# A hybrid attention step in fp32: the second feed-forward network's last six output blocks, walked one token half at a time

## The reference, cut to what matters

```python
def rmsnorm(x, g):
    y = xf * lax.rsqrt(jnp.mean(xf * xf, axis=-1, keepdims=True) + RMS_EPS)
    return (y * g).astype(x.dtype)

h = x + 0.5 * swiglu(rmsnorm(x, g_ffn1), w1g, w1u, w1d)
h = h + mix                      # attention, not touched here
h = h + 0.5 * swiglu(rmsnorm(h, g_ffn2), w2g, w2u, w2d)
y = rmsnorm(h, final_norm)
```

## Time and profile before

| | |
|---|---|
| Median of 3 runs | 1061.3 us (1061.2, 1061.3, 1063.53) |
| Profiled execution, its own time | 1062.71 us |
| Its span in the trace | 1060.9 us |
| TensorE busy, share of the span | 98% |
| VectorE, ScalarE, GpSimd busy | 79%, 51%, 8% |
| Granted TensorE clock, mean | 0.994 of full |

### The profile page before, as it was taken

The page is one execution under the profiler, slowest core; times in us unless marked ns, Lnnn a source line. Parts: engine busy times, 40 slices in busy tenths (PEclk is TensorE's granted clock), DMA queues, the critical chain, the costliest instruction groups (busy, mean ns, idle before and its releaser), DMA issues. The chain is left out here.

```text
span 1060.9 us, 19168 instructions
## 1 busy us (share of the span) xinstructions
PE 1039.9 (98%) x7698; PEld 1008.7 (95%) x7698; DVE 835.1 (79%) x1257; ACT 539.8 (51%) x929; POOL 86.7 (8%) x84
## 2 busy tenths in 40 slices
PE   9999999999999999988999999999999999999996
PEld 9999999999999999977888889999999999999996
DVE  6999988999878463377777766699998899987744
ACT  7536645666455443344344444544664666645532
POOL 0000000000000034022322102200000000000022
PEclk9999999999999999999999999999999999999998
DMA  5222223223231335220112212213222322223122
GB/s 210 82 80 93 107 82 117 81 87 113 80 120 41 100 114 198 69 86 1 51 50 71 75 41 73 87 40 120 106 94 81 116 84 98 102 80 120 60 61 90
DMA packets 22663, 94.45 MB, mean 89 GB/s; under 512 B 2928, under 2 KB 6000, under 8 KB 16048
## 3 DMA queue, kind: packets, MB, share of 16 engines
q1 hardware_dynamic: 22576, 93.23, 25.4%
HBM read 88.24 MB, written 4.98 MB: 88 GB/s over the span
## 5 line engine op out<-in xcount | busy, mean ns | idle before, releaser
L808 PE MATMUL acc<-c_hi,w_lo 128*128 128x288 f32 x952 | 282.0, 296 | 0.0
L808 PE MATMUL acc<-c_hi,w_hi 128*128 128x288 f32 x952 | 281.1, 295 | 0.0
L808 PE MATMUL acc<-c_lo,w_hi 128*128 128x288 f32 x952 | 277.6, 292 | 0.0
L1564 DVE TENSOR_TENSOR w_lo<-raw,w_hi 128x1024 fp32r<-128x1024 f32 (+3 forms) x161 | 176.4, 1096 | 57.0 <-ACT w_hi L1149 54.3
L808 PEld LDWEIGHTS acc<-c_lo,w_hi 128*128 128x128 f32 x952 | 180.8, 190 | 0.0
L808 PEld LDWEIGHTS acc<-c_hi,w_hi 128*128 128x128 f32 x952 | 179.1, 188 | 0.2
L808 PEld LDWEIGHTS acc<-c_hi,w_lo 128*128 128x128 f32 x952 | 178.6, 188 | 0.0
L1149 ACT ACTIVATE w_hi<-raw 128x1024 fp32r<-128x1024 f32 (+3 forms) x161 | 145.5, 904 | 38.3 <-PE acc L943 17.2
L1297 ACT ACTIVATE comb<-acc 128x288 f32<-128x288 f32 x200 | 82.4, 412 | 151.4 <-PE acc L808 147.4
L1564 DVE TENSOR_TENSOR w_lo<-comb,w_hi 128x1024 fp32r<-128x1024 f32 x100 | 122.1, 1221 | 43.7 <-ACT w_hi L1167 43.7
L808 PE MATMUL acc<-h_hi,w_lo 128*128 128x288 f32 x448 | 132.7, 296 | 0.0
(11 more groups left out here) (222 smaller groups left out, 1699.8 us busy)
## 6 DMA issues: line engine op xcount, KB each, us to landing
raw<-in_w1st SPq DMA_DIRECT2D x17, 1024.0 KB, 4.8
raw<-in_w2st SPq DMA_DIRECT2D x17, 1024.0 KB, 4.8
raw<-in_w1sd SPq DMA_DIRECT2D x8, 1024.0 KB, 4.8
raw<-in_w2sd SPq DMA_DIRECT2D x8, 1024.0 KB, 4.8
raw<-in_w_qk SPq DMA_DIRECT2D x13, 512.0 KB, 3.5
raw<-in_w1gu SPq DMA_DIRECT2D x10, 512.0 KB, 4.6
raw<-in_w2gu SPq DMA_DIRECT2D x10, 512.0 KB, 3.7
raw<-in_w_out SPq DMA_DIRECT2D x8, 512.0 KB, 4.5
```

Source lines behind the costliest of these rows:

```text
L808: m = nc.tensor.matmul(acc[:, banks[side_of(p)], 0:HALF], w_part[:, col:col + P], x_part, start=n in (P1, P5, P2) and k == 0 and e == 0, s ...
L1564: return nc.vector.tensor_tensor(cols, src, hi.bitcast(FP32), ALU.subtract).then_inc(split_ready, 1)
```

## The change

For the second network, output blocks 2 to 7 (`HALVED` = 2 and up) are walked twice: all six for token half 0, then all six for token half 1. So that the split weights of all six last for both passes, they go into the memory of `c_hi` and `c_lo` (6 x 768 columns of each) and no longer into `w_hi` and `w_lo`; their split waits only for the last period's products. The number of products, their shapes, the loads and the splits stay as they are. The additions into `res`, the squares and GpSimd's additions of these blocks become half as wide and twice as many. The column sums of half 0 are issued after block 2 of the second pass, its spread after block 4, and the scaling and stores of half 0 are placed among the second pass. The waits for a free bank are by half: block d from 4 on waits for the same half of block d-2 to be added.

```diff
 SPLIT_X, SPLIT_Y, SPLIT_Z = 0, 2176, 1024
+HALVED = 2
...
+def late(key):
+    return key[0] == "dn" and key[1] == 1 and key[2] >= HALVED
 def split_free(key):
     kind = key[0]
+    if late(key):
+        return UNIT[("st", 1, KF - 1)] + PARTS
...
+        def split_cols(key):
+            width = block_width(key)
+            if late(key):
+                at = (key[2] - HALVED) * width
+                return tuple(c[:].rearrange("p j c n -> p (j c n)")[:, at:at + width] for c in (c_hi, c_lo))
+            at = split_base(key)
+            return w_hi[:, at:at + width], w_lo[:, at:at + width]
+        def half_out(t, d):
+            return DOWNS_BEFORE[1] + HALVED + (KD - HALVED) * t + d - HALVED + 1
+        def half_added(t, d):
+            return 3 * KD + HALVED + (KD - 1 - HALVED) * t + d - HALVED
...
-                for d in range(2, KD - (1 if ffn_no else 0)):
-                    down_block(ffn_no, d)
+                if ffn_no == 0:
+                    for d in range(2, KD):
+                        down_block(ffn_no, d)
+            def down_token_half(t, d):
+                key = ("dn", 1, d)
+                if t == 0:
+                    block_ready(key)
+                if d < HALVED + 2:
+                    wait_down_bank(1, d)
+                else:
+                    pe.wait_ge(res_ready, half_out(t, d - 2))
+                hi, lo = split_cols(key)
+                tok = slice(t * HALF, (t + 1) * HALF)
+                for k in range(TAIL):
+                    for n, (w_part, x_part) in enumerate(((hi, h_hi), (hi, h_lo), (lo, h_hi))):
+                        m = nc.tensor.matmul(acc[:, down_bank(d) + t, 0:HALF], w_part[:, k * P:(k + 1) * P],
+                                             x_part[:, k, tok], start=k == 0 and n == 0, stop=k == TAIL - 1 and n == 2)
+                m.then_inc(down_half, 1)
+            def last_down_blocks():
+                for d in range(HALVED, KD):
+                    down_token_half(0, d)
+                for d in range(HALVED, KD):
+                    down_token_half(1, d)
+                    if d == HALVED:
+                        final_sums(0)
+                    elif d == HALVED + 2:
+                        final_spread(0)
                 final_sums(1)
                 final_spread(1)
-                if t == 0:
-                    pe.wait_ge(ssq_added, KD * 4 - 1)
+                pe.wait_ge(ssq_added, half_added(t, KD - 1))
                 pe.wait_ge(last_sq, t + 1)
...
-                base, width = split_base(key), block_width(key)
-                hi_cols(w_hi[:, base:base + width], raw[:, raw_at(key):raw_at(key) + width], key, split_free(key))
+                hi_cols(split_cols(key)[0], raw[:, raw_at(key):raw_at(key) + block_width(key)], key, split_free(key))
...
-                for d in range(KD):
-                    if d + 2 < KD:
-                        hi_block(("dn", ffn_no, d + 2))
-                    elif ffn_no == 0:
-                        hi_block(("qk", d - (KD - 2)))
-                    if ffn_no == 0 or d < KD - 1:
+                if ffn_no == 0:
+                    for d in range(KD):
+                        if d + 2 < KD:
+                            hi_block(("dn", ffn_no, d + 2))
+                        else:
+                            hi_block(("qk", d - (KD - 2)))
                         residual_next(2 * ffn_no + 1, d, DOWNS_BEFORE[ffn_no])
...
-            for d in range(Y_GP):
-                nc.scalar.activation((gate, up)[d][:], res[:, d, :], ACT.Copy,
-                                     scale=gains[:, 3, d:d + 1]).then_inc(y_scaled, 1)
-            for t in range(2):
+            def half_square(t, d):
                 tok = slice(t * HALF, (t + 1) * HALF)
-                act.wait_ge(res_ready, DOWNS_BEFORE[1] + KD + t)
-                if t == 0:
-                    act.wait_ge(ssq_added, 4 * KD - 1)
-                nc.scalar.activation(sq[:, tok], res[:, KD - 1, tok], ACT.Square).then_inc(last_sq, 1)
+                act.wait_ge(res_ready, half_out(t, d))
+                act.wait_ge(ssq_added, half_added(t, d))
+                nc.scalar.activation(sq[:, tok], res[:, d, tok],
+                                     ACT.Square).then_inc(last_sq if d == KD - 1 else sq_ready, 1)
...
+            def final_row(t):
+                tok = slice(t * HALF, (t + 1) * HALF)
                 act.wait_ge(spread, 4 + 2 * t)
                 nc.scalar.activation(rrow[:, tok], acc[:, COPY_BANK + t, 0:HALF], ACT.Copy).then_inc(final_r, 1)
+            for d in range(KD):
+                if d < KD - HALVED:
+                    hi_block(("dn", 1, d + HALVED))
+                if d < HALVED:
+                    residual_next(3, d, DOWNS_BEFORE[1])
+                else:
+                    half_square(0, d)
+                if d == KD - HALVED - 1:
+                    for e in range(Y_GP):
+                        nc.scalar.activation((gate, up)[e][:], res[:, e, :], ACT.Copy,
+                                             scale=gains[:, 3, e:e + 1]).then_inc(y_scaled, 1)
+            half_square(1, HALVED)
+            final_rms(0)
+            half_square(1, HALVED + 1)
+            half_square(1, HALVED + 2)
+            final_row(0)
+            for d in range(HALVED + 3, KD):
+                half_square(1, d)
+            final_rms(1)
+            final_row(1)
...
-                base, width = split_base(key), block_width(key)
-                lo_cols(w_lo[:, base:base + width], raw[:, raw_at(key):raw_at(key) + width],
-                        w_hi[:, base:base + width], GROUP[key])
+                hi, lo = split_cols(key)
+                lo_cols(lo, raw[:, raw_at(key):raw_at(key) + block_width(key)], hi, GROUP[key])
...
-                for d in range(KD):
+                for d in range(KD if ffn_no == 0 else HALVED):
                     if d + 2 < KD:
                         lo_block(("dn", ffn_no, d + 2))
-                    elif ffn_no == 0:
+                    else:
                         lo_block(("qk", d - (KD - 2)))
-                    elif d == KD - 1:
-                        break
...
-            def last_output(t):
+            def half_output_added(t, d):
                 tok = slice(t * HALF, (t + 1) * HALF)
-                dve.wait_ge(last_half, t + 1)
-                nc.vector.scalar_tensor_tensor(out=res[:, KD - 1, tok], in0=acc[:, down_bank(KD - 1) + t, 0:HALF], scalar=0.5,
-                                               in1=res[:, KD - 1, tok], op0=ALU.mult, op1=ALU.add).then_inc(res_ready, 1)
+                dve.wait_ge(down_half, (KD - HALVED) * t + d - HALVED + 1)
+                nc.vector.scalar_tensor_tensor(out=res[:, d, tok], in0=acc[:, down_bank(d) + t, 0:HALF], scalar=0.5,
+                                               in1=res[:, d, tok], op0=ALU.mult, op1=ALU.add).then_inc(res_ready, 1)
...
-            last_output(0)
+            lo_block(("dn", 1, 2 * HALVED))
+            for d in range(HALVED, KD):
+                half_output_added(0, d)
+                if d + HALVED + 1 < KD:
+                    lo_block(("dn", 1, d + HALVED + 1))
+            half_output_added(1, HALVED)
+            half_output_added(1, HALVED + 1)
             last_roots(0)
-            last_output(1)
+            half_output_added(1, HALVED + 2)
             dve.wait_ge(spread, 5)
-            dve.wait_ge(res_ready, DOWNS_BEFORE[1] + KD + 1)
-            for d in range(Y_GP, KD - 2):
+            dve.wait_ge(res_ready, half_out(0, KD - 1))
+            for d in range(Y_GP, Y_GP + 3):
                 scaled(0, d)
+            half_output_added(1, HALVED + 3)
+            for d in range(Y_GP + 3, KD):
+                scaled(0, d)
+            half_output_added(1, HALVED + 4)
+            half_output_added(1, HALVED + 5)
             last_roots(1)
-            for d in range(KD - 2, KD):
-                scaled(0, d)
             dve.wait_ge(spread, 7)
+            dve.wait_ge(res_ready, half_out(1, KD - 1))
             for d in range(Y_GP, KD):
                 scaled(1, d)
...
-                for d in range(KD - 1 if norm == 3 else KD):
+                for d in range(HALVED if norm == 3 else KD):
...
-            gp.wait_ge(y_scaled, Y_GP)
-            for part in range(2):
-                gp.wait_ge(final_r, part + 1)
-                tok = slice(part * HALF, (part + 1) * HALF)
+            def half_sums(t, d):
+                tok = slice(t * HALF, (t + 1) * HALF)
+                gp.wait_ge(sq_ready, half_added(t, d) + 1)
+                gp.wait_ge(ssq_added, half_added(t, d))
+                nc.gpsimd.tensor_tensor(ssq[:, tok], ssq[:, tok], sq[:, tok], ALU.add).then_inc(ssq_added, 1)
+            for d in range(HALVED, KD - 1):
+                half_sums(0, d)
+            for d in range(HALVED, HALVED + 3):
+                half_sums(1, d)
+            gp.wait_ge(y_scaled, Y_GP)
+            final_scaled(0)
+            for d in range(HALVED + 3, KD - 1):
```

(29 more changed lines are left out.)

## The result

| | before | after |
|---|---|---|
| Median (7 runs each) | 1062.86 us | 1066.26 us |
| Lowest, highest | 1061.06, 1063.53 | 1064.60, 1068.71 |
| Ratio | | 1.0039, 95% interval 1.0024 to 1.0054 |
| Profiled execution, time and span | 1062.71, 1060.9 us | 1066.14, 1064.3 us |
| Granted clock, mean | 0.994 | 0.994 |

The changed kernel is slower. The two profiled executions, both with a mean clock of 0.994 and both with one early fall of the clock, at 24 us, differ by 3.4 us in span and in time. Where these 3.4 us lie can be read off four stretches.

A forecast was written before the change was run, and what follows sets the result against it. TensorE, 98% busy, was taken to bound the kernel. Stalls 3.39 plus spread 0.95 less tail 1.0 gave +3.3 us, 3.4 with half the late start; on 1061.3 that forecast 1064.7 us, range 1062.8 to 1067.0.

The forecast's parts named there:

- the base: Median of the kernel before, 1061.3 us, to which the forecast added 3.4 us.
- Stalls: First pass: TensorE waits for split weights and free banks before blocks 3 to 7, 3.39 us in all.
- The first two: First pass: waits before block 3 (low split, 0.89 us) and block 4 (low split and bank's addition, 1.69 us).
- the loop: First pass, VectorE and ScalarE: addition, square, high split, low split repeat every 2.67 us; bounds 2.57 and 3.16.
- the three later stalls: First pass, before blocks 5, 6 and 7: 0.27 us each, 0.81 us in sum.
- Spread in the stream: Second pass: half 0's spread now takes TensorE time among the products, 0.95 us; bounds 0.75 and 1.24.
- Tail: Behind the last product: half 1's square no longer waits for ScalarE's copy of half 0's spread, 1.0 us won.
- Second pass without a stall: Second pass: weights are present and VectorE has one 0.46 us addition per 2.40 us, so TensorE never waits.
- The fall in the first pass: Rival: TensorE's idle 0.89 and 1.69 us lower the clock in the first pass; +5.1 us, 1066.4, chance 0.18.
- The full cost of the overlap: Rival: any low split overlapping GpSimd loses 0.6 us, loop 3.16; +1.5 us more, 1066.2, chance 0.08.
- The full clock in the tail: Rival: clock still full at half 1's spread, making it 1.05 us shorter; +2.3 us, 1063.6, chance 0.2.
- No stall at all: Rival: the first pass does not stall, leaving 0.95 - 1.0; 1061.3 us, chance 0.06.

The follow-up runs named there:

- the doubled spread: Changed kernel with both matmuls of half 0's spread issued twice: 1065.81 us, ratio 1.0032 to the kernel before.
- the kernel before with the same tail: Kernel before plus half 1 squared before the copy, roots one scaling earlier, spread banks swapped, GpSimd's blocks stored last, 4 unread matmuls: 1062.92 us, 0.9992.
- the splits ahead: Changed kernel with splits of blocks 2 to 4 ahead of the first addition, later ones a block earlier: 1062.75 us, 0.9991; again 1063.12 us, 0.9994.
- busy matmuls: On the splits ahead: half 1's spread banks swapped, GpSimd's blocks stored last, 3 and 4 unread matmuls in TensorE's tail: 1059.66 us, 0.9973.
- a shorter tail: The splits ahead with half 1's spread banks swapped, GpSimd's blocks stored last: 1061.73 us, 0.9985; then also busy matmuls: 1059.66 us, 0.9973.

## Why the prediction was right or wrong

**The sum held; the base it was set on did not.** Forecast +3.4 us in the span, measured +3.4 (1064.3 against 1060.9). By terms:
- Stalls: 3.39 forecast, 3.24 measured. The first two, read off rows of the kernel before that the change leaves alone, came as forecast but for late starts: 0.91 for 0.89 and 1.77 for 1.69. The term of the difference that was mis-sized is the loop: 2.57 us, not 2.67. I had charged the low split 0.10 for its last overlap of 0.1 us with GpSimd, by the rule that the first to start keeps the ports to its end; the row shows 0.96, as alone. The lower of my bounds was the right one, and the three later stalls are 0.17 each, not 0.27.
- Spread in the stream: 0.95 forecast, 0.97 measured, and doubled by its experiment.
- Tail: 1.0 forecast, 0.96 measured.
- Second pass without a stall, transfers in time, table load and scalings hidden: as forecast. (One sum in it is off: a load that goes out at about 1024.5 and takes 3.2 lands at 1027.7, not 1027.9; nothing hung on it.)

**The step that failed is the last one of the sum, the base.** I put the +3.4 on a median of three, 1061.3, where the forecast of the profiled execution, 1062.71 + 3.4 = 1066.1, stood beside it and came out at 1066.14. I noted that this execution lay 1.4 above the median without asking why. The reason stood in the earlier trace rows: it had a fall of the clock at 24 us, which two of the three, by their times, had not. The median of three was one of the executions without an early fall, and those are the fewer: 16 of 78 in the experiments. The kernel before has its median at 1062.86 (7 runs) to 1063.54, and the changed one at 1065.80 to 1068.46. So the level was 1.6 us too low, 1064.7 for 1066.26; set against the kernel before as measured beside it, 1062.86, the forecast amounts to +1.8 us where +3.4 was measured. The difference was right in its mechanism and its size. That 1066.26 lay inside the range of 1062.8 to 1067.0 is in part luck: the range was drawn for rivals in the changed stretch, and executions on the level of two early falls (up to 1069.0) lie above it, a case that no rival held.

**The rivals.** The fall in the first pass didn't come in any profile of the changed kernel, and came when the stall before block 4 was made 3.0 us; for the executions that weren't profiled it stays open. The full cost of the overlap didn't come, nor did any. The full clock in the tail didn't come in the result: the clock fell at about 1055.2, 3.0 us after the last product and 0.8 ahead of the spread, where before it had been 4 and 0.6. The changed kernel's three profiles have 2.30, 2.30 and 1.94 for that spread. It was there in full with the doubled spread (1.25) and in the kernel before with the same tail (1.24), in part with the splits ahead (1.70) and with busy matmuls (1.84). No stall at all came only with the splits ahead, by an edit: 0.1 to 0.2 us under the kernel before.

**What the change earned.** Its gain is small by nature: 1.0 us of tail for 0.97 us of spread in the stream. A third of the gain was to be had by exchanging two instructions on ScalarE. The walk by halves was clearly faster than the kernel before only with the splits ahead and a shorter tail (0.9985 and 0.9973).

## What to carry to other kernels

Halving the unit of work on the engine that bounds doubles the pace at which its inputs are wanted; before such an edit, take the latency of the loop that makes them (here split, addition, square, split) from the trace and set it against the new pace, even where each engine in it is half idle. Memory freed for inputs pays when the code that fills it is moved ahead as well. Work taken out of a tail is worth what the chain behind the last product loses, less what it costs in the full stream.

## What the runs showed of the hardware

- The same program's executions lie on levels by how often and where the granted clock falls: at 24, 454 or 491 us in one execution and not in the next, for about 1.6 us (24 or 454) and 2.4 us (491). The wait of 2.0 us at 492 us ended with a fall lasting some 7 us in one profile of the changed kernel, and with none in the two others.
- A VectorE instruction that starts 0.08 us ahead of a GpSimd instruction keeps it standing: 1.54 us instead of 0.80. With GpSimd 0.69 us ahead the VectorE instruction is the one that grows, 0.96 to 1.55. Where it starts in the last 0.10 to 0.12 us of GpSimd's, it doesn't grow (0.96).
- A first matmul behind a wait starts 0.04 to 0.15 us after what it waited for ended (0.05 behind the low split of block 3, 0.14 behind the addition before block 4), against 0.02 to 0.04 for the vector engines.
